# Mixer attention of a two-layer encoder step: probabilities normalised before their transposes, and the transposes one step later

## The reference

```
s = einsum('bqhd,bkhd->bhqk', q, k) * ATTN_SCALE
s = s + dq[..., :, None] - dk[..., None, :]
s = where(k_pos[None, :] <= q_pos[:, None], s, NEG_INF)
p = softmax(s, axis=-1)                      # exp(s - max) / sum
out = einsum('bhqk,bkhd->bqhd', p, v)
```

## Time and profile before

| | |
|---|---|
| time, median of 3 runs | 2334.61 us (2332.95 to 2337.45) |
| span of the profiled execution | 2335.4 us |
| PE busy in it | 2273.7 us (97%) |
| DVE, ACT, POOL busy | 1577.4, 964.8, 299.3 us |
| TensorE's granted clock | 0.9 or more of full speed in each fortieth of the span |

### The profile page before, as it was taken

One profiled execution on the slowest core, in us unless ns is written; L12 is line 12 of the kernel. 1 busy time (PEld: TensorE's weight loads), 2 busy tenths in 40 slices (PEclk: granted clock), 3 DMA queues, 4 the chain that ended last, 5 costly groups with the idle time before them and its releaser, 6 DMA issues.

```text
span 2335.4 us, 45344 instructions
## 1 busy us (share of the span) xinstructions
PE 2273.7 (97%) x18566; PEld 2174.2 (93%) x18566; DVE 1577.4 (68%) x2863; ACT 964.8 (41%) x2081; POOL 299.3 (13%) x362
## 2 busy tenths in 40 slices
PE   8999999999998999999999999999899999999999
PEld 6999999978887999999999999998788889999999
DVE  5588858666667756667576786767666677888623
ACT  4222233455566522223342222334555564555523
POOL 0000002321103400001220000123211143000000
PEclk9999999999999999999999999999999999999999
DMA  8355645422223145455524564551333331333322
GB/s 272 117 170 172 179 124 167 122 75 81 76 78 101 37 125 154 138 143 156 145 64 140 170 178 143 150 149 45 108 111 102 92 93 46 85 97 103 97 76 72
DMA packets 392799, 277.66 MB, mean 119 GB/s; under 512 B 11137, under 2 KB 349857, under 8 KB 392593
## 3 DMA queue, kind: packets, MB, share of 16 engines
q1 hardware_dynamic: 385792, 254.77, 37.7%
q0 software_dynamic: 6800, 19.99, 3.0%
HBM read 263.48 MB, written 12.81 MB: 118 GB/s over the span
## 4 chain that ended last, share of the span: by engine, by line
PE 85%; DVE 8%; issue 2%; DMA 2%; ACT 2%; SPq 1%; POOL 0%; DVEq 0%; ACTq 0%; POOLq 0%
PE lin L1219 55%; PE lin L1576 10%; PE lin L1415 7%; PE lin L1239 2%; PE ps_s L1630 2%; PE ps_o L1711 2%; PE ps_t L1652 1%; DVE acc L2499 1%; PE ps_s L1415 1%; DMA raw<-in_ffn_w_down 1%; DVE w_lo L2377 1%; SPq L971 1%; PE ps_t L1599 1%; DVE h_lo L2616 1%; PE ps_s L1295 1%
## 5 line engine op out<-in xcount | busy, mean ns | idle before, releaser
L2377 DVE TENSOR_TENSOR w_lo<-raw,w_hi 128x1024 fp32r<-128x1024 f32 (+1 forms) x272 | 331.2, 1221 | 190.4 <-ACT w_hi L1826 189.5
L1219 PE MATMUL lin<-h_hi,w_hi 128*128 128x272 f32 x2096 | 453.1, 289 | 2.8 <-DVE w_lo L2377 2.0
L1219 PE MATMUL lin<-h_hi,w_lo 128*128 128x272 f32 x2096 | 450.7, 288 | 0.0
L1219 PE MATMUL lin<-h_lo,w_hi 128*128 128x272 f32 x2096 | 449.2, 288 | 0.0
L1826 ACT ACTIVATE w_hi<-raw 128x1024 fp32r<-128x1024 f32 (+1 forms) x272 | 280.2, 1038 | 200.9 <-DMA raw<-in_ffn_w_down 147.9
L1219 PEld LDWEIGHTS lin<-h_hi,w_hi 128*128 128x128 f32 x2096 | 335.6, 188 | 4.8 <-issue 2.6
L1219 PEld LDWEIGHTS lin<-h_lo,w_hi 128*128 128x128 f32 x2096 | 335.9, 188 | 0.0
L1219 PEld LDWEIGHTS lin<-h_hi,w_lo 128*128 128x128 f32 x2096 | 334.0, 189 | 0.0
L2499 DVE SCALAR_TENSOR_TENSOR acc<-raw,silu_c,acc 128x512 f32<-128x512 f32 x448 | 312.6, 756 | 0.0
L1219 PE MATMUL lin<-act_hi,w_hi 128*128 128x272 f32 x1280 | 280.6, 289 | 4.4 <-DVE w_lo L2377 4.1
L1219 PE MATMUL lin<-act_hi,w_lo 128*128 128x272 f32 x1280 | 277.8, 288 | 0.0
(11 more groups left out here) (424 smaller groups left out, 4266.5 us busy)
## 6 DMA issues: line engine op xcount, KB each, us to landing
raw<-in_w_ada SPq DMA_DIRECT2D x128, 512.0 KB, 3.9
raw<-in_ffn_w_gate SPq DMA_DIRECT2D x88, 512.0 KB, 4.1
raw<-in_ffn_w_up SPq DMA_DIRECT2D x88, 512.0 KB, 3.9
raw<-in_ffn_w_down SPq DMA_DIRECT2D x64, 448.0 KB, 4.2
raw<-in_ffn_w_down SPq DMA_DIRECT2D x32, 512.0 KB, 5.2
raw<-in_w_in_ab SPq DMA_DIRECT2D x24, 512.0 KB, 3.8
raw<-in_w_in_c SPq DMA_DIRECT2D x24, 512.0 KB, 3.8
start_w<-in_w_ada SPq DMA_DIRECT2D x16, 512.0 KB, 11.9
```

What stands on the lines that cost most here:

```text
L1219: m = nc.tensor.matmul(out[a], w_tile(w, k), mv[:, k0 + k, half(a)], start=first and k == 0 and n == 0, stop=last and k == u["tiles"] - 1 ...
L2377: nc.vector.tensor_tensor(w_all(w_l, u["tiles"]), src, w_all(w_h, u["tiles"]).bitcast(F32), ALU.subtract).then_inc(lo_done, 1)
```

## The change

In stages a and c DVE multiplies each probability tile by its reciprocal sum (`scale_probs`) right behind the reciprocal, in step j + 2, and the transposes of tile j wait for that product. `lag` becomes 3 in all stages; with it tr0 to tr9, the copies, pair0 to pair4 and the turns (steps 5, 9, 13 in place of 4, 8, 12) come one step later, and the last quarter of the third projection (lin11) is cut into two halves in steps 11 and 12. `inv_wide`, its turn, `inv_t` and the multiplying `take` go in stages a and c: ACT writes `o_hi` from PSUM itself, and DVE's `out_lo` reads PSUM. Stages b keep their order.

```diff
-TURN_STEPS = {"a": (4, 8, 12), "c": (4, 8, 12), "b": (5, 9, 13), None: (4, 8, 12)}
+TURN_STEPS = {"a": (5, 9, 13), "c": (5, 9, 13), "b": (5, 9, 13), None: (5, 9, 13)}
...
-            if st.att == "b":
-                return {11: (0,), 12: (1,)}.get(s, ())
-            return (0, 1) if s == 11 else ()
+            return {11: (0,), 12: (1,)}.get(s, ())
...
-            return (1, 4, 12) if ahead(st) else (4, 8, 13 if st.att == "b" else 12)
+            return (1, 4, 12) if ahead(st) else (4, 8, 13)
...
-            lag = 3 if st.att == "b" else 2
+            lag = 3
...
-                        pe.wait_ge(exp_done, st.at("s") + j + 1)
+                        pe.wait_ge(prob_scaled, 2 * st.at("inv") + j + 1)
...
-                def turn_inverse(n):
-
-                    t = order[2 * n][0]
-                    r = rows(t)
-                    pe.wait_ge(inv_spread, st.at("inv") + n + 1)
-                    pe.wait_ge(o_read, st.at("pv") + n)
-                    nc.tensor.transpose(ps_o[:, (2 + n % 2) * P:(2 + n % 2) * P + r], inv_wide[0:r, n % 2, :],
-                                        ident[0:r, 0:r])
-
                 def pair_values(n):
...
+                    if n >= 1:
+                        pe.wait_ge(o_lo_done, st.at("ot") + n)
...
-                def inv_copy(q):
...
                 def out_hi(q):
...
-                    act.wait_ge(o_read, st.at("pv") + q + 1)
-                    nc.scalar.activation(o_hi[:, st.tile_of(-1), t * P:t * P + r], o_nat[:, q % 2, 0:r], ACT.Copy)\
+                    act.wait_ge(pv_done, st.at("pv") + q + 1)
+                    nc.scalar.activation(o_hi[:, st.tile_of(-1), t * P:t * P + r],
+                                         ps_o[:, (q % 2) * P:(q % 2) * P + r], ACT.Copy)\
...
+                def scale_probs(j):
+
+                    t = order[j][0]
+                    r, n = rows(t), keys(t)
                     dve.wait_ge(inv_done, st.at("s") + j + 1)
-                    pair = row_inv[0:r, j - 1:j + 1].rearrange("p (h o) -> p h o", o=1)
-                    nc.vector.tensor_copy(inv_wide[0:r, n % 2, :].rearrange("p (h d) -> p h d", h=2),
-                                          pair.broadcast_to([r, 2, HD])).then_inc(inv_spread, 1)
+                    nc.vector.tensor_scalar(probs[0:r, j % PSLOTS, 0:n], probs[0:r, j % PSLOTS, 0:n],
+                                            row_inv[0:r, j:j + 1], None, ALU.mult).then_inc(prob_scaled, 1)
...
                     j = s - 2
                     if 0 <= j < 10:
                         invert(j)
-                        if att == "b" and j % 2:
+                        if att != "b":
+                            scale_probs(j)
+                        elif j % 2:
                             combine(j // 2)
```

More of the change, by code:

```diff
@@ L370, in program @@
         work = sb("work", [P, 2, TOK])
-        inv_wide = sb_at("inv_wide", [P, 2, P], F32, work_at)
         sums_at = cursor[0]
@@ L499, in program @@
         probsT = sb("probsT", [P, 2, QT, P])
-        o_nat = sb("o_nat", [P, 2, P])
-        inv_t = sb("inv_t", [P, 2, P])
+        o_nat = sb("o_nat", [P, P])
         mixer_top = cursor[0]
@@ L651, in program @@
         ot_ps = sem("ot_ps")
-        inv_out = sem("inv_out")
-        inv_spread = sem("inv_spread")
+        prob_scaled = sem("prob_scaled")
         o_hi_done = sem("o_hi_done")
@@ L1562, in stage @@
                 evs = st.ev()
-                lag = 3 if att == "b" else 2
+                lag = 3
                 def lin_chunk(s, part_half):
@@ L1667, in values @@
                     if q >= 1:
-                        pe.wait_ge(o_read, st.at("pv") + q)
+                        pe.wait_ge(o_read, st.at("comb") + q)
                     if t == QT:
@@ L1765, in stage @@
                     if att != "b" and 0 <= j < 10 and j % 2:
-                        turn_inverse(j // 2)
                         pair_values(j // 2)
@@ L2285, in b_square @@
                     r = rows(t)
-                    act.wait_ge(o_read, st.at("pv") + q + 1)
+                    act.wait_ge(o_read, st.at("comb") + q + 1)
                     act.wait_ge(b_sq_done, 5 * st.tile_of(-1) + q)
-                    nc.scalar.activation(o_nat[0:r, 0, :], b_nat[0:r, st.tile_of(-1), t, :], ACT.Square,
+                    nc.scalar.activation(o_nat[0:r, :], b_nat[0:r, st.tile_of(-1), t, :], ACT.Square,
                                          accum_out=b_sq[0:r, st.tile_of(-1), t:t + 1]).then_inc(b_sq_done, 1)
@@ L2313, in stage @@
                         split(("o", st.j, 4))
-                    j = s - lag - 2
+                    j = s - lag
+                    if 0 <= j < 10 and (j % 2 if att == "b" else True):
+                        empty_probs(j, j // 2 if att == "b" else j, lag)
+                    j = s - lag - 1
                     if att != "b" and 0 <= j < 10 and j % 2:
                         out_hi(j // 2)
[L2317 to L2325, removed]
                     j = s - lag - 2
@@ L3025, in take @@
                     r = rows(t)
[L3026 to L3033, removed]
+                    dve.wait_ge(pv_done, st.at("pv") + q + 1)
+                    nc.vector.tensor_copy(b_nat[0:r, st.tile_of(-1), t, :], ps_o[0:r, (q % 2) * P:(q % 2) * P + P])\
+                        .then_inc(o_read, 1)
                 def out_lo(q):
@@ L3039, in out_lo @@
                     c = slice(t * P, t * P + r)
-                    nc.vector.tensor_tensor(o_lo[:, st.tile_of(-1), c], o_nat[:, q % 2, 0:r],
+                    nc.vector.tensor_tensor(o_lo[:, st.tile_of(-1), c], ps_o[:, (q % 2) * P:(q % 2) * P + r],
                                             o_hi[:, st.tile_of(-1), c].bitcast(F32), ALU.subtract).then_inc(o_lo_done, 1)
@@ L3060, in stage @@
                         add_bias(s)
-                    if att != "b" and 0 <= j - 1 < 10 and j % 2 == 0:
-                        out_lo((j - 1) // 2)
                     if att != "b" and 0 <= j < 10 and j % 2:
-                        take(j // 2)
+                        out_lo(j // 2)
                     if att == "b" and st.st == 8 and s in (1, 3, 5):
```

3 lines of the change are left out of this document (removed).

## The result

The changed kernel takes 2360.3 us (median of 4 runs, 2359.67 to 2365.07) where the kernel before took 2336.03 beside it (4 runs, 2332.95 to 2339.40). The ratio is 1.0110, interval 1.0098 to 1.0122: 24.3 us slower by the medians, 25.7 by the ratio. The profiled execution took 2359.67 with a span of 2357.9, so that the spans differ by 22.5 us. The forecast was +18.8, or 2353.5.

A forecast was written before the change was run, and what follows sets the result against it. PE, busy 97% and serving its queue in order, was taken as the bound. Terms 11.9 + 4.4 + 2.1 + 0.9 - 0.5 = +18.8 us gave a 2354.2 span, 2353.5 median; own range 2348 to 2359, 8 in 10 2343 to 2361.

The forecast's parts named there:

- 0.9 later: Stage C1: gain at the front eaten up by turn1 behind ACT's exponential of tile 8; 0.9 us longer, perhaps off by 1.5.
- Turned reciprocals, 9.1 us: TensorE's queue: 60 matmuls go, five in each of 12 stages, 0.76 us a stage by distances between starts, 9.1 us saved.
- The rival that a turn is worth its whole record: Part of the half-size case (17%): each of 60 turns saves 287 ns, 17.2 us, 8.1 more than booked.
- turn0 +0.74: First turn behind pair0: uncovered round trip over ACT's copy of tile 2, new wait 0.73 to 0.75 us.
- turn1 +0.55: Second turn, behind pair2: uncovered round trip over ACT's copy of 128 columns, new wait 0.55 us.
- tr8 +0.6: Tile 8's transposes, now next to tr7, wait for ACT's copy: 0.76 against 0.11 to 0.2, new wait 0.6 us.
- lin4's wait: Step 2: DVE's weight split later, TensorE at lin4 earlier; wait grows 0.65 us in C, 0.15 in A, 0.8 in A7.
- changed shapes: Halved lin11 and transposes now ending before scores instead of a projection: 0.2 us a stage in all.
- Slack wins: Rival: the three round trips hidden and lin4's split in time, some -8 us, 2326.5; chance 5%.
- no change: Rival: round trips of turn0 and tr8 covered after all in 11 stages, +4 us, 2338.6; chance 8%.
- Slower still: Rival: DVE's queue late at more places than lin4, 0.15 us more per pair of tiles, 9 us, 2362; chance 12%.
- the sentence on the page of the skill: Skill's 275 ns per transpose would make 60 turns worth 16.5 us, the sum +11 us in place of +18.5.

The follow-up runs named there:

- The order alone: Kernel before with transposes and turns one step later in stages a and c, reciprocals still turned, no product: 2368.81 against 2338.98, ratio 1.0135.
- the four edits: Changed kernel with turn0/turn1 inside lin6/lin10, tile 8's transposes in ps_o, lin4's second weight split before tile 2's bias, ACT's tile 0 copy before its exponential: 2338.30, ratio 1.0003.
- the split moved alone: Changed kernel with DVE's second half split of lin4's weights ahead of the bias of tile 2 in stages a and c: 2360.76 against 2335.98, ratio 1.0106.
- the turns moved alone: Changed kernel with turn0 and turn1 between the halves of lin6 and lin10 in stages a and c: 2363.99 against 2337.41, ratio 1.0111.
- the two covers: Changed kernel with turn0 and turn1 between the halves of lin6 and lin10, and tile 8's transposes in the free half of ps_o: 2343.61 against 2337.41, ratio 1.0028.

## Why the prediction was right, and where not

- *Direction and mechanism: right; size: too small.* The order of TensorE's queue costs more than the turned reciprocals give. The order alone is +31.6 us; the four edits against its waits bring the kernel back to before. The time, 2360.3, is 6.8 us over the forecast and just over its own range of 2348 to 2359.
- *The step that failed is C1, "0.9 later" in the sum.* It was +3.98, outside the 1.5 that I allowed for. The premise was that the step more is a help there, since other work now stands in front of the waits. Up to lin8 nothing was gained: before, tr0, tr1 and lin8 waited 2.5 us there; after, the scores wait 0.26, tr0 1.33 for its product and lin8 1.38 for DVE's split, 3.0 in all, and lin8 starts 0.78 later in the stage. The wait at lin8 belongs to the order: 2.25 us with the order alone, 1.94 without products. Behind it come 5.45 us for what C5 does in 3.00, at the lower clock, a term that the sum put at nothing. Then turn0 waits 0.95, and turn1 1.85 for ACT, whose copy stands behind an exponential and a split (the wait foreseen, not its price). That stretch's 2.45 isn't all lost, since later waits shrink by a part of it: filling the waits of C1 shortened it by 1.02. How the other 2 of the 3.1 divide among the waits wasn't tested; the walk isn't written out, so that it can't be said which of its terms was short.
- *From the forecast to the time.* On the profiled spans it is 22.5 for 18.8: +3.1 in C1, +1.0 up to C1, +0.7 in C2 to C7, -1.0 from C8 on. The +1.0 is luck: -1.80 ahead of the stages and +2.2 at the lower clock in stage 8, for which nothing was booked, nearly cancel. Of the rest of the 6.8, 1.4 is that before has a median of 2336.03 here and had 2334.61 when I forecast, and 1.8 is that the medians are 24.3 apart and the two profiled executions 22.5.
- *Turned reciprocals, 9.1 us:* 10.1 measured. The rival that a turn is worth its whole record fell.
- *turn0 +0.74, turn1 +0.55:* 0.74 and 0.53 in C5. *tr8 +0.6:* tr8 starts 0.68 after tr7, where 0.76 was worked out; the price by distances is about the 0.6. *lin4's wait:* TensorE waits 0.63, its weight load 0.86 where 0.31 before, so it grew by 0.55 and not 0.65. In A1, A3 and A5 TensorE doesn't wait at lin4 at all. A middle stage C is +2.08 for +1.98 and an A stage +1.8 for +1.48, so what was booked as changed shapes, 0.2, must be some 0.4 to 0.5; that is a remainder, and no run splits it.
- The product takes 0.49 us, not 0.55, at 512 columns, and 0.29 at 128; DVE is busy 22 us more, not 30.
- *The rivals.* "Slack wins" and "no change" fell with the waits in their places. "Slower still" named 2362, nearer to the time than my forecast, but its reason (DVE late at every tile) isn't what happened: in the changed kernel the transposes wait for this product once, in C1, and without products a stage is 0.26 us shorter. It is what happens with the transposes left at two steps, +82 us.
- *A slip:* the sentence on the page of the skill starts from +18.5; the sum is +18.8.
- *Open:* when the clock falls. Two waits in C1 were enough in some kernels and not in others, and the same code has a fall in one execution and none in the next (stage 8 of layer 0). The times go with it: of 21 runs of before, the three with a mean clock of 0.999 took 2333.7 to 2335.4 us, the four with 0.995 took 2338.6 to 2342.3. So one profile of a kernel can't tell how much of its 24 or 26 us is the clock's.

## What to carry to other kernels

Where an engine is busy 97% and serves its queue in order, price a reordering by what stands between each wait and its release, tile by tile; a removed instruction is worth its distance between starts. Work that only moves can cost more than work that goes: in a middle stage C three waits for one shared PSUM tile, two of 0.74 and 0.53 and one of some 0.6, cost over twice the 0.76 that five matmuls gave. And if a wait is taken away, look on every engine for what was hidden under it: the split moved alone, the turns moved alone, gave nothing; the two covers, the split and the copy together gave 22 us by the medians and 25 by the ratios, which is break-even with before and not yet the gain that the removed matmuls were meant to bring. Last, where the time depends on the clock, compare a stage over several profiles before its length is put down to an edit.

## What the runs showed of the hardware

- After two waits of 1.3 us with 0.7 us of work between them the granted clock was 0.50 for 2.0 us and 0.56 for the next 3.9. Matmuls of 128x272 then follow each other at 0.45 us per two, in place of 0.25. With the waits filled by transposes it stayed at 1.00. With the second cut to 0.27 us it stayed at 1.00 in one kernel and fell in another, where matmuls of 128x272 were again 0.45 us apart.
- The same code had a granted clock of 0.91 over 37.8 us in one execution and 1.00 over 35.4 us in another (stage 8 of layer 0).
- A product of fp32 tiles with one scalar for each partition in SBUF takes DVE 0.49, 0.42, 0.35 and 0.29 us at 512, 384, 256 and 128 columns.
- A round trip from TensorE over ACT's copy of one PSUM tile and back takes 0.68 us with a copy of 128 columns, transposes included.
